# Moving work between stages and engines of a two-block transformer kernel: score products, rotary part, low-rank head and gates

## What is computed

```python
out_fox = _causal_softmax_attention(fq, fk, fv, head_scale, f_cum)
out_sb = _stick_breaking_attention(sq, sk, sv, head_scale)
out_mla = _causal_softmax_attention(q_full, k_full, v_mla, mla_scale)
out_mem = einsum(softmax(mem_logits), mv)
mixed = concatenate([out_fox, out_sb, out_mla, out_mem])
h_res = _layer_norm(DEEPNORM_ALPHA * h_res + (mixed * silu(gate)) @ w_out[l], ln_g[l], ln_b[l])
```

```python
h = rms_norm(x, norm_mix_pre) * (1.0 + sc1) + sh1
proj = h @ w_in
o_attn = dilated_attention_mixer(q, k, v, positions)
o_rwkv = rwkv7_mixer(r, k, v, dw, da, dg, ...)
merged = sigmoid(g_attn) * (o_attn @ wb[:256]) + sigmoid(g_rwkv) * (o_rwkv @ wb[256:])
x = x + gt1 * rms_norm(merged @ w_out, norm_mix_post)
x = x + gt2 * rms_norm(square(relu(h2 @ w_ff1)) @ w_ff2, norm_ffn_post)
```

## Time and profile before

| | us |
|---|---|
| median of 3 runs | 4343.93 (4343.72 to 4348.23) |
| profiled execution | 4336.1 |
| its span | 4334.3 |
| TensorE busy | 3935.7 |
| VectorE, ScalarE, GpSimd busy | 1691.4, 1131.1, 510.3 |
| branches, 3081.4 to 3443.7 | 362.3 |
| stick-breaking attention, per layer | 120.8 and 120.0 |
| window projection and rotary part, 1745.9 to 2045.5 | 299.6 |

### The profile page before, as it was taken

How to read it: one execution, slowest core, us unless ns; L and a number is a source line. 1 busy time by engine, 2 the same in 40 slices (tenths; PEclk the granted TensorE clock), 3 DMA queues, 4 the chain that set the end, 5 groups by cost and what they waited for, 6 DMA issues and landing times. The chain is left out here.

```text
span 4334.3 us, 65941 instructions
## 1 busy us (share of the span) xinstructions
PE 3935.7 (91%) x28854; PEld 2720.9 (63%) x28854; DVE 1691.4 (39%) x2995; ACT 1131.1 (26%) x2159; POOL 510.3 (12%) x160
## 2 busy tenths in 40 slices
PE   5889989998898897897779999999899999999998
PEld 4664667976464687365635555555566647787876
DVE  6634545445355344104723444444111134132243
ACT  1426333014544311000623333333100022010011
POOL 2110013210100130003000000000000002322331
PEclk9999999999998999999889999999899999999999
DMA  3121101222020120100010000000121101111112
GB/s 140 40 88 35 61 30 49 80 88 69 20 76 20 49 88 40 69 30 0 1 52 23 18 18 18 18 12 22 54 80 43 37 20 59 49 49 45 43 49 107
DMA packets 165310, 204.60 MB, mean 47 GB/s; under 512 B 20190, under 2 KB 142624, under 8 KB 162728
## 3 DMA queue, kind: packets, MB, share of 16 engines
...
## 5 line engine op out<-in xcount | busy, mean ns | idle before, releaser
L2804 PE MATMUL banks<-h_channel_major,pair_weights 128*128 128x512 f32 x768 | 391.5, 625 | 0.3 <-ACT x_residual L3195 0.3
L208 PE MATMUL banks<-h_high,weights_high 128*128 128x512 f32 x608 | 240.9, 396 | 5.1 <-PEq L809 5.1
L208 PE MATMUL banks<-h_high,weights_low 128*128 128x512 f32 x608 | 238.4, 392 | 0.0
L193 POOL CAST weights_high<-weights_value 128x2048 fp32r<-128x2048 f32 x34 | 68.3, 2009 | 1346.1 <-DMA weights_value<-in_w_in_dram 705.6
L208 PE MATMUL banks<-ffn_in_high,ffn_weights_high 128*128 128x512 f32 x512 | 204.4, 399 | 14.1 <-PEq L75 14.1
L208 PE MATMUL banks<-ffn_in_low,ffn_weights_high 128*128 128x512 f32 x512 | 202.9, 396 | 0.0
L208 PE MATMUL banks<-ffn_in_high,ffn_weights_low 128*128 128x512 f32 x512 | 202.9, 396 | 0.0
L208 PE MATMUL banks<-ffn_weights_high,hidden_high 128*128 128x512 f32 x512 | 199.5, 390 | 3.1 <-ACT hidden_value L3762 3.1
L208 PE MATMUL banks<-ffn_weights_low,hidden_high 128*128 128x512 f32 x512 | 199.2, 389 | 0.0
L208 PE MATMUL banks<-ffn_weights_high,hidden_low 128*128 128x512 f32 x512 | 199.2, 389 | 0.0
L2804 PEld LDWEIGHTS banks<-h_channel_major,pair_weights 128*128 128x128 f32 x768 | 129.4, 190 | 102.8 <-issue 90.4
...
## 6 DMA issues: line engine op xcount, KB each, us to landing
...
```

Of the source, the lines that this page charges most:

```text
L193: nc.gpsimd.tensor_copy(high, value).then_inc(rounded, 1)
L208: mm = nc.tensor.matmul(out, x, y, start=(first and i == 0 and j == 0), stop=(last and i == n - 1 and j == 2))
L2804: mm = nc.tensor.matmul(bank, wr[:, n % R_TILES, c, :], k.ht[:, c, half * HALF:(half + 1) * HALF], start=(c == 0), stop=(c == KT - 1))
```

## The change

It touches ten places.

1. First edge: GpSimd starts splitting weights after VectorE has normalised four tiles.
2. `sb_project`: value tiles 6 and 7 and the load of `C_CKV` leave the stage.
3. `stick_attention`: scores are made once, in one of three slots, and the tail sums are added on top of them; the two late value tiles are multiplied at `it == 1`, into banks 6 and 7, and moved by VectorE; SP then loads `C_CKV`.
4. `pair_attention`: ScalarE scales the first head's weights, VectorE the second's.
5. Last edge: from group 16 on the output groups go by token tile; statistics, root, norm, square and diagonal are made per tile; the turning is cut into units of four, two, four and two tiles and starts a group earlier.
6. `window_project` and `window_rope` become one block: TensorE turns tile i - 1 behind the projection of tile i, ScalarE moves all results, VectorE multiplies by sine and cosine and adds. GpSimd has nothing there.
7. `window_attention` loads the low-rank weights and four tiles of the pairs' weights into places that are free by then, and its TensorE program ends with the 32 low-rank products. The block `low_rank` is gone; its copies, shift, tanh and sigmoid open the block `pairs`, where TensorE starts with the projection of k.
8. `rwkv` ends by loading two chunks of gate weights.
9. `branches` (class `Gates`, new) works channel-major in 16 units of one channel tile and a half of the tokens: 8 + 2 plain products of 512 columns and 48 split ones for both gates. GpSimd splits the weights of each channel tile, ScalarE and VectorE split h once at the start. In the last channel tile the gates come ahead of the plain products. x and the output weights are loaded at the end.
10. `mix_out` projects from `merged` as it is, and GpSimd's first split for the feed-forward waits for the last projection. In `FeedForward` only addresses change.

Its core, by place:

Stick-breaking attention (`stick_attention`): one product instead of two, three slots, and the late value groups.

```diff
     def z(u):
-        return k.psum[:, 2 * (u % 2):2 * (u % 2) + 2, first[u]:HALF]
+        return logs(u)
 
     def logs(u, c0=None, c1=HALF):
-        return k.psum[:, 4:6, first[u] if c0 is None else c0:c1]
+        return k.psum[:, 2 * (u % 3):2 * (u % 3) + 2, first[u] if c0 is None else c0:c1]
...
+            def do_scores(u):
+                if u >= 3:
+                    pe.wait_ge(weights_ready, u - 2)
...
-                    mm = nc.tensor.matmul(to[:, e, :], kt[half_rows[e], p, b * P:(b + 1) * P],
...
-                if u >= 2:
-                    pe.wait_ge(softplus_ready, u - 1)
-                products(u, z(u), True).then_inc(scores_done, 1)
+                    mm = nc.tensor.matmul(z(u)[:, e, :], kt[half_rows[e], p, b * P:(b + 1) * P],
+                                          qt[half_rows[e], p, half * HALF + first[u]:(half + 1) * HALF], start=True, stop=True)
+                mm.then_inc(scores_done, 1)
 
             def do_tails(u):
-                if u:
-                    pe.wait_ge(weights_ready, u)
-                products(u, logs(u), False)
                 pe.wait_ge(softplus_ready, u + 1)
...
                     do_scores(it)
+                if it == 1:
+                    for i, (t, pairs, dst) in enumerate(late):
+                        gemm(nc, k.bank(6 + i, 256), pairs).then_inc(values_done, 1)
...
+                nc.vector.tensor_copy(late[i][2], k.bank(6 + i, 256)).then_inc(values_moved, 1)
```

```diff
             def scale(u):
-                for e in range(2):
...
-                    last.then_inc(scaled, 1)
+                n_rows = len(units[u][1])
+                dve.wait_ge(exp_done, 2 * u + 1)
+                nc.vector.reciprocal(column(inverse, u, 0, 0, n_rows), column(total, u, 0, 0, n_rows)).then_inc(inverse_ready, 1)
+                dve.wait_ge(exp_done, 2 * u + 2)
+                step(nc.vector.reciprocal(column(inverse, u, 1, 0, n_rows), column(total, u, 1, 0, n_rows)))
+                for i, t, at, n in rows_at(u):
+                    x = cols(weights, u, 1, at, n)
+                    last = nc.vector.tensor_scalar_mul(x, x, column(inverse, u, 1, i))
...
+            def scale_first(u):
+                act.wait_ge(inverse_ready, u + 1)
+                act.wait_ge(exp_done, 2 * u + 1)
+                for i, t, at, n in rows_at(u):
+                    x = cols(weights, u, 0, at, n)
+                    last = nc.scalar.mul(x, x, column(inverse, u, 0, i))
```

```diff
     def out_group(g):
+        if not b and g >= 16:
+            return g % 4, g // 4
...
+    mix_units = ([((0, 4), c) for c in range(KT)] + [((4, 6), c) for c in range(4, KT)] + [((4, 8), c) for c in range(4)]
+                 + [((6, 8), c) for c in range(4, KT)])
+    mix_on_dve = [n % 2 == 1 and not 8 <= n < 12 for n in range(len(mix_units))]
...
+            if mem:
+                pool.wait_ge(normed, 4)
...
+                    if g in (20, 24, 28):
+                        tile_moments(g // 4 - 1)
+                    if g in (24, 28):
...
+                    if g in (21, 25, 29):
+                        tile_root(g // 4 - 1)
...
+                        make_diagonals(0, 4)
+                    if g in (25, 29):
+                        make_diagonals(g // 4 - 2, g // 4 - 1)
```

```diff
-    project_stage(k, "sb_project" + tag, groups, W, loads=(C_SV,), splits=(C_SV,), prefetch=(C_CQ, C_CKV),
-                  clear=b.forget_here, nbanks=7, rider=condition(0), rows_after=(3, 5, 6, 7, 10, 13))
+    project_stage(k, "sb_project" + tag, groups, W, loads=(C_SV,), splits=(C_SV,), prefetch=(C_CQ,),
+                  clear=b.forget_here, nbanks=7, rider=condition(0), rows_after=(3, 5, 6, 7, 9, 11))
+    late_values = [(t, over_columns(b, C_SV, t, 0, 256), values[:, t, :]) for t in range(NT - 2, NT)]
```

```diff
+            for i in range(TILES):
+                project(i)
+                if i:
+                    if i == 1:
+                        pe.wait_ge(here, 48)
+                    rotate(i - 1)
+            for n in range(WINDOW_GROUPS * NT):
+                values(n)
+                if n == 1:
+                    rotate(TILES - 1)
...
+            for j in range(2):
...
+                for h in range(2):
+                    mm = gemm(nc, k.bank(4 + 2 * j + h), [(low_weights(i // 4)[:, i % 4, j * P:(j + 1) * P],
+                                                           k.ht[:, i, h * HALF:(h + 1) * HALF]) for i in range(KT)])
+                mm.then_inc(early.low_done, 1)
```

```diff
             def project(p):
 
                 for i, j in enumerate(J_ORDER):
+                    if p == 0 and i == 1:
+                        yield from low_rank(0)
...
             def front_steps(p):
-                if p == 0:
-                    yield from low_rank(0)
...
                 elif is_front:
-                    low_sigmoids(0)
+                    for j in range(2):
+                        act.wait_ge(k.early.low_done, j + 1)
+                        nc.scalar.copy(raw[j][:, 4:4 + S], k.banks2(4 + 2 * j)).then_inc(raw_kept, 1)
+                    act.wait_ge(raw_mixed, 2)
+                    nc.scalar.activation(low[0:64, 0, :], low[0:64, 0, :], ACT.Tanh).then_inc(low_ready, 1)
+                    nc.scalar.activation(low[:, 1, :], low[:, 1, :], ACT.Sigmoid).then_inc(low_ready, 1)
```

```diff
-                gemm(nc, k.bank(2 * (g % 4)), [(k.ht[:, j, tok], wg[i][:, j, :, :].rearrange("p a c -> p (a c)")) for j in range(KT)])
...
+            def gate(c, half):
...
+                for i in range(2):
+                    mm = gemm(nc, k.bank(4 * half + 2 + i), [((gates.high[c % 2][:, j, i, :], gates.low[c % 2][:, j, i, :]),
+                                                              (part(gates.h_high, j, half), part(gates.h_low, j, half)))
+                                                             for j in range(KT)])
+                mm.then_inc(gates_done, 1)
...
+            for c in range(LAST):
+                for half in range(2):
+                    room(c, half)
+                    of_rwkv(c, half)
+                    of_attention(c, half)
+                    gate(c, half)
+            for half in range(2):
+                room(LAST, half)
+                gate(LAST, half)
+            for half in range(2):
+                of_attention(LAST, half)
+            for half in range(2):
+                of_rwkv(LAST, half)
...
+                nc.gpsimd.tensor_copy(gates.high[s][:], gates.value[s][:]).then_inc(w_rounded, 1)
+                pool.wait_ge(w_rounded, c + 1)
+                nc.gpsimd.tensor_tensor(gates.low[s][:], gates.value[s][:], gates.high[s][:], ALU.subtract).then_inc(w_split, 1)
...
+                nc.vector.tensor_tensor(gates.h_low[:, j, :], k.ht[:, j, :], gates.h_high[:, j, :], ALU.subtract).then_inc(h_split, 1)
...
-            for n in range(2 * KT):
-                turn_merged(n)
...
+            pool.wait_ge(products, NT)
```

642 lines of the change are left out of this document (377 added, 265 removed).

## The result

The changed kernel takes **4199.1 us** (median of 4 runs, 4192.4 to 4205.9), the kernel before beside it 4343.8 (4341.0 to 4348.2): ratio 0.9666, 95% interval 0.9648 to 0.9684. It is 145 us faster, where 196 were forecast, and the time lies above the range of the prediction (4120 to 4186). In the profiled runs the span went from 4334.3 to 4196.3, 138.0 less.

The account below looks back on a forecast made before the run. TensorE, busy 91% of the span, was taken as the bound: save products or close its idle stretches. Nine items summed to 195.8 us, taken from the median 4343.9 to give 4148, range 4120 to 4186.

Parts of the forecast that it names:

- Item 3: Stick-breaking attention, two layers: dropping the second score products saves 17.1 a layer, net 15.7; about 32 us (22 to 44).
- ten units' worth of columns, 9.5: Stick-breaking attention: the 16 diagonal units save 9.5 us a layer, beside 7.6 from eight full units.
- Item 4: Paired attention, six stages: ScalarE taking half of VectorE's scaling gains 4 us in all (-6 to 14).
- Item 1: First edge: GpSimd waits for four normalised tiles, so TensorE begins 17.6 us earlier; saves 16.6 (15 to 17.6).
- Items 2, 6, 7: Value products and edge before stick-breaking, 24.6; window projection and rotary stage, 21.5; window attention to first pair, 40.8 us.
- Item 8: Branches: 16 units of 19.7 us replace 362.3, less 12.4 for a worse start; saves 34.7 (25 to 46).
- Item 5: Last edge: work by token tile and turning a group earlier save 16 us (12 to 19).
- Item 9: Mix-out: turns and idle go, a start of 3.2 stays, 3 lost to a late addition; saves 5.6 (3 to 9).
- hand-overs come back: Rival: stick-breaking units take 5.15, not 4.75; paired attention loses; branches' start costs 5 more; 4177 us, chance 0.17.
- slower: Rival: split products make TensorE stand at every gate in the branches, clock at 1.2 GHz; 119 us slower, 4463, chance 0.02.

Follow-up runs that it names:

- both waits attacked: Changed kernel with GpSimd's second stick-breaking split held to the fifth unit and scores one place earlier, read in kernels with further edits; 4169.8 us with four edits.
- its own two runs: VectorE scaling both heads again in the changed kernel, 4195.4 us; ScalarE scaling the first head in the kernel before, 4360.0 against 4348.5.
- the combined kernels: Changed kernel with VectorE's scaling, late split, early scores and filled last pair, 4169.8 us; plus late root, 4165.7; plus 24 small products, 4173.4.
- part 4 alone: The kernel before with only ScalarE scaling the first head's weights in the six paired stages; 4360.0 us against 4348.5, ratio 1.0026.
- a loop with a sum of stretches of 10.2: Pair loop of the changed kernel with the second score products back in stick-breaking attention (two score slots, one for tail sums); 4202.7 us.
- the second profile of before: The kernel before, unchanged, profiled again; 4343.0 us in its one run, span 4341.2.

## Why the prediction was wrong

By its own items, in profiled time (the sum 195.8, measured 138.0):

- **Item 3 (32, got 16.9)** is the largest miss of a term. The steady unit was right (4.75, measured 4.84). The step that failed is the sum of 17.1 a layer, "ten units' worth of columns, 9.5" in it: it took removed busy time for saved time in every unit. The narrow units gave their share, but where a full unit follows one of 128 columns, ScalarE's and VectorE's steps behind the scores are longer than TensorE's work beside them; it waits 2.1 to 2.7 there, its clock falls, and the step gets 0.2 to 1.7 longer instead of 0.95 shorter. Putting the products back costs 5 to 7 a layer, not 17. The charge of 2.5 for GpSimd's split was too small as well: 2.81 of wait and a half-speed stretch behind it. With both waits attacked the two stages come to 212.7, 28 saved: the term was within reach of this idea, but not of this code.
- **Item 4 (+4, got -14.2)**. "ScalarE's own copies come 0.7 us later, into its idle time" failed. Per last unit the copies come 1.6 later (four scalings of 128x256 take 1.75) and TensorE waits for them, and its clock falls behind that wait. The part costs 5.6 to 7.6 by its own two runs and some 10 by the combined kernels, at or beyond the low end given (-6), and the gain of 4 did not come. Another 4 us of the 18 missing is the kernel before, whose profile had its luck in the first latent attention.
- **The pair loop (0, got -16.5)** had no term. I took code that the change leaves alone as unchanged in time. 7 of it lie in the first seven pairs, 4 in busy time at a lower granted clock and 3 in idle time; the kernel before with part 4 alone loses 9 there, nearly all by the clock, without any edit near them. 6 to 9 lie in the last pair: longer stretches that nothing releases, and more time at the low clock. Shown: filling the waits brings the clock back and most of the time; one stretch per pair stands at a fixed place of the whole program and not of the loop. Open: what causes it, what decides where in the first seven pairs the clock dips, and how much of the loop's length hangs on either, since a loop with a sum of stretches of 10.2 took 802.2 all the same.
- **Item 1 (16.6, got 13.2)**: TensorE began at 23.45 as forecast, but "end some 1 us too late at worst" missed ScalarE, whose root of the memory rows now stands ahead of four evacuations. With the root moved, the edge saves 17.8.
- **Items 2, 6, 7** (24.6, 21.5, 40.8; got 25.0, 22.2, 42.1) held, and with them the way they were worked out: products counted at 0.86 or 0.118, and edges at 0.8 to 2.
- **Item 8** (34.7, got 32.2): the start was sized well. The stage begins at 2978.14, where ScalarE and GpSimd start, so of TensorE's 11.16 idle only 7.4 lie in it (7.1 charged), and the wait for h is 2.6 (5.3 charged). What the sum had at nothing is the clock behind these two waits: the first unit's own work takes 24.2 instead of 19.8, its first products at a granted clock of 0.78. The running unit is 19.78 instead of 19.7.
- **Item 5** (16, got 13.7): waits of 2.60, 1.56 and 3.31 stay in the last edge.
- **Item 9** (5.6, got 3.9): the late addition cost 3.3 (3 charged), and the first twelve groups of products take 84.0 instead of 82.5.
- **The baseline**: the prediction added 7.8 us for the median over the profiled run and used the profile's stages as they were. With the second profile of before (4341.2) the sum of what was gained is 144.9, as by the medians.

The rival "hand-overs come back" had the right mechanism for items 3 and 4, and put it at 29 (4177): it sized ScalarE as the bound of each full unit, which did not come, and missed the steps behind the narrow units. With the pair loop's term on top it would have been 4193; the measured 4199.1 is above that too. That loop belonged in the range: one per cent of clock over 790 us is 8 us. The rival "slower" did not come: behind the first unit the branches ran at a granted clock of 1.00.
